# Dense weight units with the low-weight products last, and a mixture-of-experts run that ends without a gather for a step that doesn't follow

## The chip, the cores and the metric

One NeuronCore of a Trainium2 chip. The metric is the device time of one execution in microseconds (us). The engines are TensorE (PE; its weight loads are listed as PEld), VectorE (DVE), ScalarE (ACT), GpSimd (POOL) and SyncE (SP), which issues nearly all DMAs. They run in parallel, each in its own program order, and meet at semaphores only.

## The reference

A trunk of two layers on 256 tokens of 1024 channels, all in float32. Each layer is a token mixer and a channel mixer, both with a norm before and after:

```
h = rms_norm(x, mix_pre_g) * (1 + sc_m) + sh_m
y = hybrid_mixer(h, ...)          # z = h @ w_in; convolution, stick-breaking attention, gated linear attention;
                                  # (g_a * y_a + g_b * y_b + g_c * y_c) @ w_o
x = x + g_m * rms_norm(y, mix_post_g)
h = rms_norm(x, ffn_pre_g) * (1 + sc_f) + sh_f
y = swiglu(h)                     # layer 0: dense, 2816 wide
y = moe_swiglu(h)                 # layer 1: 8 experts, 3584 wide, the best 2 for each token
x = x + g_f * rms_norm(y, ffn_post_g)
```

## The kernel before

**Weights in units.** All weights come from HBM as units of 128 x 2048 floats (1 MB) into six raw buffers, in the fixed order of PLAN for the dense part, then 42 units for each of 8 experts. To reach float32 accuracy with fp32r products, ACT writes the high part of a unit (w_hi, line 592, in the expert part 841) and DVE subtracts it from the raw one for the low part (w_lo, line 990, then 1303). The operand from the activations is split likewise. Every product is then three: high x high, high weights x low activations, low weights x high activations. hi_written counts ACT's parts, raw_taken DVE's (which also frees the raw buffer for SP's next load), consumed counts units that PE has finished (which frees the slot of w_hi and w_lo). There are four slots; the weights of slots 2 and 3 lie in the tensor acts, the others in tensors named w_hi and w_lo.

**The dense part.** PE walks through the units in order. Each takes 48 products (128 x 128 weights, 256 columns), made by project (line 1587), project_tokens (1667), project_branch (1679) or project_down (1697), and each begins with begin(u): wait for raw_taken, then for the PSUM bank. The three products of one chunk follow each other. In each mixer, units 0 to 29 are the columns of w_in, 30 to 35 the outputs of the three branches ("out"), 36 to 39 the columns of w_o ("wo"). The functions hook(layer, i) put the attention, convolution and norm work between units by number. The first eight units of w_in in layer 0 go another way: project_rows (line 1653) runs over all 16 columns with w_hi and high activations, waits, then with w_lo, then with w_hi and low activations.

**Merging the branches.** DVE's merge (lines 1241 and 1245) multiplies each out unit by its gates, POOL adds the first two branches (line 567), and DVE adds the third once POOL's sum is there (line 1245). ACT takes the high part (line 662), DVE the low part (line 1292, counted by s_split). Unit 36 needs both, in four pieces.

**The expert part.** A step is one expert on at most 128 of its tokens. gather(step, half) (line 1994) picks the tokens with a selection matrix that DVE writes (select, line 1395); ACT and DVE split the result (949, 1468). Gate and up units (1959) and down units (1974) follow, the latter summed in banks 5 and 6 over the whole step; turn (1984) transposes the activations, ACT and DVE split them (944, 1461: ae_split). After the last tile of a step PE gathers for the next step, then runs the last two down units. The result is split by ACT and DVE (957, 1476), and scatter (2014, 2015) spreads it back over the tokens in four products p, which DVE adds up (1484). After 8 steps, over_steps (line 464) runs as many more as there are experts with more than 128 tokens; the count is read from memory by every engine, and here it is 0. Then comes the last scatter, ACT's squares (972), their sums on PE (1558), a root (608, 609), and DVE's update of x (1091, 1095), which SP stores.

Of the kernel before, what the change touches and what calls it, by code (L numbers as in the profile page):

```python
# [205 lines left out]
def program(nc, x_t, vecs, c_row, glr_w, a2, router, stream, experts, out_t):  # L206
    with ExitStack() as ctx:
# [152 lines left out]
        first_gate = sem("first_gate_ready")  # L360
        first_high = sem("first_h_high")
# [216 lines left out]
        def _(act):  # L578
# [338 lines left out]
            def expert_step(step, expert, first=False):  # L917
# [20 lines left out]
                for half in range(2):  # L938
                    input_high(step + 1, half)
# [25 lines left out]
            with act.Fori(1, N_EXP) as g:  # L965
                expert_step(g, g)
            n_steps = over_steps(act, expert_step)
# [10 lines left out]
        def _(dve):  # L978
# [507 lines left out]
            def expert_step(step, expert, first=False):  # L1486
# [24 lines left out]
                else:  # L1511
                    dve.wait_ge(list_ready, 1)
                    column = column_of(step + 1)
                select(column, sel, chosen_f, sel_ready)
                select(column, sel_w, weights_f, sel_w_ready)
# [3 lines left out]
                for half in range(2):  # L1519
                    split_input(step + 1, half)  # L1520
# [15 lines left out]
            with dve.Fori(1, N_EXP) as g:  # L1536
                expert_step(g, g)
            n_steps = over_steps(dve, expert_step)
# [6 lines left out]
        def _(pe):  # L1545
# [24 lines left out]
            def begin(u):  # L1570
                pe.wait_ge(raw_taken, POS[u] + 1)
# [5 lines left out]
            def project(u, hi, lo, ready=None, before=0, chunks=1):  # L1577
# [4 lines left out]
                for k in range(KC):  # L1582
                    if ready is not None:
                        pe.wait_ge(ready, before + k // chunks + 1)
                    for c in range(2):
                        for n, (w, high) in enumerate(parts(s)):
# [3 lines left out]
                                           stop=(k == KC - 1 and n == 2), skip_group_check=True)  # L1590
                mm.then_inc(consumed, 1)
# [68 lines left out]
            def project_tokens(u, hi, lo):  # L1660

                s = begin(u)
                out = two(bank[BANKS[u][0][0]])
                for t in range(2):
                    for k in range(KC):
                        for n, (w, high) in enumerate(parts(s)):
                            mm = pe.matmul(out[:, t, :], (hi if high else lo)[:, k, P * t:P * t + P],  # L1667
                                           w[:, 256 * k:256 * k + 256],
# [487 lines left out]
```

## Time and profile before

| | |
|---|---|
| median of 3 runs | 1792.62 us (1791.63 to 1792.68) |
| profiled execution, own time | 1791.98 us |
| its span, first to last instruction | 1790.2 us |
| PE busy | 1761.6 us (98%) |
| DVE busy | 1523.5 us (85%) |
| ACT busy | 1137.0 us (64%) |
| HBM read | 522.65 MB, 293 GB/s over the span |
| mean granted TensorE clock | 0.997 |

The profile is of one execution; times within it count from its first instruction. A busy share says how much an engine has to do; what sets the time is read from the chain that ended last, which is followed back from the last instruction through whatever released it.

### The profile page before, as it was taken

What the parts mean: (1) busy time and instruction counts of PE and PEld (TensorE: products, weight loads), DVE (VectorE), ACT (ScalarE), POOL (GpSimd) and SP (SyncE); (2) the same over time, 40 slices, a digit from 0 to 9 for tenths busy, and PEclk for the clock granted to TensorE, in tenths of its full rate; (3) what the DMA queues carried; (4) which work ended last, traced back from release to release, by engine and by line L of the source; (5) the groups of instructions that cost most, each with busy time, mean ns of one, the idle gap of its engine ahead of it and who ended that gap; (6) DMA issues with size and microseconds to landing.
All of it is one profiled execution on the core that took longest, in us unless ns stands there. A gap on an engine that the chain in (4) does not pass through costs nothing.

```text
span 1790.2 us, 28816 instructions
## 1 busy us (share of the span) xinstructions
PE 1761.6 (98%) x10885; PEld 1560.5 (87%) x10886; DVE 1523.5 (85%) x1450; ACT 1137.0 (64%) x970; POOL 188.3 (11%) x158
## 2 busy tenths in 40 slices
PE   9999999999999999999999999999999999999997
PEld 7999989999999999868888888888888888888886
DVE  7899787999777784769898898898888988988986
ACT  5556475333464556567777777777777777777774
POOL 0395010000029400100000000000000000000000
PEclk9999999999999999999999999999999999999998
DMA  9854655999744444539989989999899899898991
GB/s 387 316 195 154 227 181 199 357 385 371 297 142 165 140 143 142 189 124 362 382 335 364 372 339 369 348 365 372 328 373 374 329 374 370 332 373 338 367 373 73
DMA packets 72818, 524.87 MB, mean 293 GB/s; under 512 B 8145, under 2 KB 8273, under 8 KB 9122
## 3 DMA queue, kind: packets, MB, share of 16 engines
q1 hardware_dynamic: 72578, 523.51, 77.0%
q8 instruction: 59, 0.97, 0.2%
q0 software_dynamic: 160, 0.23, 0.0%
q14 instruction: 21, 0.17, 0.0%
HBM read 522.65 MB, written 1.05 MB: 293 GB/s over the span
## 4 chain that ended last, share of the span: by engine, by line
PE 92%; DVE 5%; ACT 1%; issue 1%; DMA 1%; SPq 0%; DVEq 0%; ACTq 0%
PE bank L1959 34%; PE bank L1587 19%; PE bank L1974 17%; PE bank L1697 4%; PE bank L1679 3%; PE bank L1667 3%; PE bank L1653 2%; PE bank L1994 2%; PE bank L1984 1%; PE bank L1558 1%; DVE w_lo L990 1%; DVE arena L1165 1%; PE bank L1629 1%; DMA raw<-in_stream 1%; PE bank L2014 0%
## 5 line engine op out<-in xcount | busy, mean ns | idle before, releaser
L1303 DVE TENSOR_TENSOR w_lo<-raw,w_hi 128x2048 fp32r<-128x2048 f32 x224 | 509.8, 2291 | 82.6 <-ACT w_hi L841 82.6
L841 ACT ACTIVATE w_hi<-raw 128x2048 fp32r<-128x2048 f32 x224 | 428.6, 1917 | 97.2 <-PE bank L1974 70.4
L1587 PE MATMUL bank<-acts,w_hi 128*128 128x256 f32 x1760 | 311.9, 281 | 7.1 <-DVE acts L1292 3.6
L1959 PE MATMUL bank<-acts 128*128 128x512 f32 x1248 | 304.3, 392 | 0.0
L1959 PE MATMUL bank<-w_hi,acts 128*128 128x512 f32 x960 | 297.3, 391 | 0.0
L1587 PEld LDWEIGHTS bank<-acts,w_hi 128*128 128x128 f32 x1760 | 268.3, 189 | 10.3 <-DVE w_lo L990 6.5
L1303 DVE TENSOR_TENSOR acts<-raw,acts 128x2048 fp32r<-128x2048 f32 x112 | 256.1, 2287 | 20.9 <-ACT acts L841 20.6
L1959 PEld LDWEIGHTS bank<-acts 128*128 128x128 f32 x1248 | 231.2, 188 | 46.8 <-DVE acts L1303 0.4
L841 ACT ACTIVATE acts<-raw 128x2048 fp32r<-128x2048 f32 x112 | 215.1, 1921 | 72.1 <-PE bank L1959 69.8
L1974 PE MATMUL bank<-w_hi,acts 128*128 128x512 f32 x832 | 256.1, 389 | 0.0
L1587 PE MATMUL bank<-acts,w_lo 128*128 128x256 f32 x880 | 245.6, 279 | 0.0
L990 DVE TENSOR_TENSOR w_lo<-raw,w_hi 128x2048 fp32r<-128x2048 f32 x82 | 190.3, 2321 | 44.1 <-ACT w_hi L592 43.8
L592 ACT ACTIVATE w_hi<-raw 128x2048 fp32r<-128x2048 f32 x82 | 156.6, 1911 | 100.4 <-PE bank L1587 70.0
L1959 PEld LDWEIGHTS bank<-w_hi,acts 128*128 128x128 f32 x960 | 178.9, 188 | 36.3
L1959 PE MATMUL bank<-w_lo,acts 128*128 128x512 f32 x480 | 186.8, 389 | 0.0
L1974 PEld LDWEIGHTS bank<-w_hi,acts 128*128 128x128 f32 x832 | 156.2, 188 | 32.4
L1587 PEld LDWEIGHTS bank<-acts,w_lo 128*128 128x128 f32 x880 | 165.7, 188 | 0.0
L1974 PE MATMUL bank<-w_lo,acts 128*128 128x512 f32 x416 | 161.9, 389 | 0.0
L1004 DVE SCALAR_TENSOR_TENSOR raw<-raw,arena 128x1024 f32<-128x1024 f32 x96 | 114.9, 1233 | 15.5 <-DMA raw<-in_stream 10.6
L1959 PEld LDWEIGHTS bank<-w_lo,acts 128*128 128x128 f32 x480 | 90.1, 188 | 19.0
L539 POOL TENSOR_SCALAR arena<-arena 128x256 f32<-128x256 f32 x60 | 102.4, 1707 | 0.0
L1165 DVE SCALAR_TENSOR_TENSOR arena<-arena 128x256 f32<-128x256 f32 x180 | 97.6, 601 | 0.9 <-DVE arena L1215 0.3
(273 smaller groups left out, 2246.0 us busy)
## 6 DMA issues: line engine op xcount, KB each, us to landing
raw<-in_experts SPq DMA_DIRECT2D x336, 1024.0 KB, 5.1
raw<-in_stream SPq DMA_DIRECT2D x161, 1024.0 KB, 6.1
arena<-in_x_t SPq DMA_DIRECT2D x2, 512.0 KB, 4.6
out_t<-arena SPq DMA_DIRECT2D x4, 256.0 KB, 2.4
arena<-in_vecs SPq DMA_DIRECT2D x1, 224.0 KB, 5.4
arena<-in_glr_w POOLq DMA_DIRECT2D x2, 64.0 KB, 4.7
arena<-in_a POOLq DMA_DIRECT2D x2, 32.0 KB, 5.2
arena<-in_router POOLq DMA_DIRECT2D x1, 32.0 KB, 2.1
```

Source lines behind the costliest of these rows:

```text
L539: pool.tensor_scalar(product, src, w, None, ALU.mult).then_inc(pool_products, 1)
L592: act.activation(w_hi[SLOT[u]], raw[:, slot, :], ACT.Copy).then_inc(hi_written, 1)
L841: act.activation(expert_hi[s], raw[:, slot, :], ACT.Copy).then_inc(hi_written, 1)
L990: dve.tensor_tensor(w_lo[SLOT[u]], raw[:, POS[u] % RAW, :], f32(w_hi[SLOT[u]]), ALU.subtract).then_inc(raw_taken, 1)
L1004: ins = dve.scalar_tensor_tensor(w, w, 1.0, cond[row], ALU.mult, ALU.mult, accum_out=ar[:, at:at + 1])
L1165: ins = dve.scalar_tensor_tensor(acc, src, w, acc, ALU.mult, ALU.add)
L1303: dve.tensor_tensor(expert_lo[s], raw[:, slot, :], f32(expert_hi[s]), ALU.subtract).then_inc(raw_taken, 1)
L1587: mm = pe.matmul(out[:, c, :], w[:, 256 * k + P * c:256 * k + P * c + P], (hi if high else lo)[:, k, :], start=(k == 0 and n == 0 and c == 0),
L1667: mm = pe.matmul(out[:, t, :], (hi if high else lo)[:, k, P * t:P * t + P], w[:, 256 * k:256 * k + 256], start=(k == 0 and n == 0), stop=( ...
L1697: mm = pe.matmul(out[:, c % 2, :], w[:, 1024 * f + P * c:1024 * f + P * c + P], (ff_hi if high else ff_lo)[t % 2][:, f, :], start=first, s ...
L1959: mm = pe.matmul(bank[b][:, :], (xe_hi if high else xe_lo)[:, c:c + P], w[:, 512 * kk:512 * kk + 512], start=(half == 0 and kk == 0 and n ...
L1974: mm = pe.matmul(bank[5 + d][:, :], (ae_hi if high else ae_lo)[odd][:, c:c + P], w[:, 1024 * f + 512 * d:1024 * f + 512 * d + 512], start= ...
```

## The change

Five edits:

1. project, project_tokens, project_branch and project_down (but for its last unit) run in two passes over a unit: all products with w_hi first, as soon as hi_written and the bank allow, then, behind the wait for raw_taken, all with w_lo. The number of products and loads is the same.
2. Unit 36 ("wo", first) gets a function of its own, project_merged, which waits for high and low pieces of the activations apart. Units that wait for chunks keep the old order as project_chunks.
3. The last of the 8 expert steps is written out behind the loop, with ahead=False: no selection, no gather and no input split for a ninth step. An overflow step (again=True) gathers for itself at its start.
4. In a step's last down unit the halves d are outermost, and the new semaphore first_half tells ACT when bank 5 is done, so that the first half of the result can be split while PE finishes bank 6.
5. scatter waits for the two halves of the split result one by one, and the last scatter (final=True) has no wait for a next input.

```diff
+            def begin_high(u):
+                pe.wait_ge(hi_written, WPOS[u] + 1)
                 for b, before in BANKS[u]:
                     if before:
                         pe.wait_ge(bank_read[b], before)
                 return SLOT[u]
+            def begin(u):
+                pe.wait_ge(raw_taken, POS[u] + 1)
+                return begin_high(u)
+
+            def low_last(u, hi, lo):
+
+                s = SLOT[u]
+                yield w_hi[s], (hi, lo), True
+                pe.wait_ge(raw_taken, POS[u] + 1)
+                yield w_lo[s], (hi,), False
...
+            def project(u, hi, lo):
+
+                begin_high(u)
+                out = two(bank[BANKS[u][0][0]])
+                for w, parts_of_h, first in low_last(u, hi, lo):
+                    for k in range(KC):
+                        for c in range(2):
+                            for n, h in enumerate(parts_of_h):
+                                mm = pe.matmul(out[:, c, :], w[:, 256 * k + P * c:256 * k + P * c + P], h[:, k, :],
+                                               start=(first and k == 0 and n == 0 and c == 0),
+                                               stop=(not first and k == KC - 1), skip_group_check=True)
+                mm.then_inc(consumed, 1)
+
+            def project_merged(u, hi, lo, before):
+
+                s = begin(u)
+                out = two(bank[BANKS[u][0][0]])
+                for q in range(4):
+                    for n, (w, h) in enumerate(((w_hi[s], hi), (w_lo[s], hi), (w_hi[s], lo))):
+                        if n == 0:
+                            pe.wait_ge(merged_hi, before + q + 1)
+                        if n == 2:
+                            pe.wait_ge(s_split, before + q + 1)
+                        for k in (2 * q, 2 * q + 1):
...
@@ down
-                for f in range(2):
+                order = [(f, d) for f in range(2) for d in range(2)]
+                if last and half == 1:
+                    order = [(f, d) for d in range(2) for f in range(2)]
+                for f, d in order:
...
+                    if last and half == 1 and f == 1 and d == 0:
+                        mm.then_inc(first_half, 1)
                 mm.then_inc(consumed, 1)
@@ scatter
-            def scatter(step):
-
-                pe.wait_ge(ye_split, step * 2)
-                pe.wait_ge(xe_split, step * 2 + 2)
+            def scatter(step, final=False):
+
+                if not final:
+                    pe.wait_ge(xe_split, step * 2 + 2)
                 for p in range(4):
+                    if p % 2 == 0:
+                        pe.wait_ge(ye_split, step * 2 + (p // 2 - 1))
@@ expert_step on TensorE
-            def expert_step(step, expert, first=False):
+            def expert_step(step, expert, first=False, again=False, ahead=True):
+                if again:
+                    gather(step, 0)
+                    gather(step, 1)
...
-                gather(step + 1, 0)
-                gather(step + 1, 1)
+                if ahead:
+                    gather(step + 1, 0)
+                    gather(step + 1, 1)
...
-            with pe.Fori(1, N_EXP) as g:
+            with pe.Fori(1, N_EXP - 1) as g:
                 expert_step(g, g)
-            scatter(over_steps(pe, expert_step))
+            expert_step(N_EXP - 1, N_EXP - 1, ahead=False)
+            scatter(over_steps(pe, over_step), final=True)
@@ expert_result on ScalarE
-                act.wait_ge(consumed, step * EU + N_W)
                 for half in range(2):
+                    if half == 0:
+                        act.wait_ge(first_half, step)
+                    else:
+                        act.wait_ge(consumed, step * EU + N_W)
```

## Rows read from the trace of the kernel before

**Rows 1.** The page: busy time by engine, and the chain's shares by engine.

```profile
PE 1761.6 (98%) x10885; PEld 1560.5 (87%) x10886; DVE 1523.5 (85%) x1450; ACT 1137.0 (64%) x970; POOL 188.3 (11%) x158
...
PE 92%; DVE 5%; ACT 1%; issue 1%; DMA 1%; SPq 0%; DVEq 0%; ACTq 0%
```

**Rows 2.** Windows: us, busy us (instructions) by engine, granted clock, DMA.

```profile
222.00:265.00 43.00, 39.21 (x337) 38.31 (x335) 35.18 (x35) 29.91 (x25) 7.66 (x4) 1.00 0.54 187
320.00:472.00 152.00, 152.00 (x1285) 152.00 (x1284) 141.90 (x170) 54.62 (x36) 0.00 (x0) 1.00 0.97 375
...
800.00:1762.00 962.00, 962.00 (x4528) 803.39 (x4527) 860.81 (x548) 702.69 (x474) 0.00 (x0) 1.00 0.92 355
1771.20:1776.40 5.20, 3.13 (x17) 3.13 (x18) 3.35 (x5) 3.72 (x6) 0.00 (x0) 0.78 0.02 6
```

**Rows 3.** Chain that ended last, 228 to 266 us: start, us, what.

```profile
232.96 0.38 issue
...
244.47 0.84 issue
...
262.73 2.30 DVE w_lo L990
```

**Rows 4.** The same chain, 705 to 745 us.

```profile
722.77 0.42 issue
...
741.39 2.30 DVE w_lo L990
```

**Rows 5.** Timeline of DVE, 244 to 262 us: start, us, instructions, [idle before].

```profile
246.52 2.90 DVE L990 TENSOR_TENSOR w_lo<-raw,w_hi 128x2048 fp32r<-128x2048 f32 x1
...
251.04 0.69 DVE L1241 TENSOR_TENSOR arena<-bank,arena 128x512 f32<-128x512 f32 x1 [0.43 <-PE bank L1679]
...
260.14 1.47 DVE L1292 TENSOR_TENSOR acts<-arena,acts 128x512 fp32r<-128x512 f32 x2
```

**Rows 6.** Instructions of lines 567 and 1245: ns min/median/max, first and last start.

```profile
L567 POOL TENSOR_TENSOR arena<-arena x8: 1292/1300/3345, 246.0 to 729.7; 128x512 f32<-128x512 f32 x8
...
L1245 DVE TENSOR_TENSOR arena<-arena x8: 691/692/1848, 251.8 to 738.2; 128x512 f32<-128x512 f32 x8
```

**Rows 7.** Chain, pieces of three dense stretches.

```profile
27.37 17.18 PE bank L1653 x144
...
203.98 10.91 PE bank L1587 x96
...
323.68 11.31 PE bank L1587 x96
```

**Rows 8.** Timeline, 1755 to 1775 us.

```profile
1758.40 1.10 DVE L1395 TENSOR_SCALAR arena<-arena 128x128 f32<-128x128 f32 x4
...
1759.02 1.92 ACT L841 ACTIVATE w_hi<-raw 128x2048 fp32r<-128x2048 f32 x1 [0.80 <-PE bank L1974]
...
1761.62 2.28 DVE L1303 TENSOR_TENSOR w_lo<-raw,w_hi 128x2048 fp32r<-128x2048 f32 x1
...
1763.83 0.68 DVE L1461 TENSOR_TENSOR acts<-bank,acts 128x512 fp32r<-128x512 f32 x1
...
1771.85 1.29 DVE L1476 TENSOR_TENSOR acts<-bank,acts 128x512 fp32r<-128x512 f32 x2 [4.77 <-ACT acts L957]
```

**Rows 9.** Chain, 1755 to 1791 us.

```profile
1762.14 3.57 PE bank L1994 x32
1765.71 5.48 PE bank L1974 x24
...
1776.40 4.07 PE bank L1558 x16
```

**Rows 10.** Timeline of weight loads, 1770 to 1775 us.

```profile
1773.27 0.19 PEld L2014 LDWEIGHTS bank<-selection_turned,acts 128*128 128x128 f32 x1 [2.51 <-issue]
```

**Rows 11.** Instructions of line 465: ns min/median/max, first and last start.

```profile
L465 PEldq COMPARE_BRANCH  x1: 3372/3372/3372, 1768.0 to 1768.0; - x1
...
L465 DVEq COMPARE_BRANCH  x1: 63/63/63, 1767.3 to 1767.3; - x1
```

More of the change, by code:

```diff
@@ L360, in program @@
         first_gate = sem("first_gate_ready")
+        first_half = sem("expert_first_half")
         first_high = sem("first_h_high")
@@ L915, in silu_tile, with over_step @@
                 act.activation(silu_e[odd], bank[2 * odd][:, :], ACT.Silu).then_inc(silu_done, 1)
-            def expert_step(step, expert, first=False):
+            def over_step(step, expert):
+                expert_step(step, expert, again=True, ahead=False)
+            def expert_step(step, expert, first=False, again=False, ahead=True):
+                if again:
+                    for half in range(2):
+                        input_high(step, half)
                 for k in range(4):
@@ L937, in expert_step @@
                 tile_high(step, 0, FT - 1)
-                for half in range(2):
-                    input_high(step + 1, half)
+                if ahead:
+                    for half in range(2):
+                        input_high(step + 1, half)
             def tile_high(step, odd, t):
@@ L1484, in add_result, with over_step, expert_step @@
                     dve.tensor_tensor(to, to, SCATTER[p][:, :], ALU.add).then_inc(moe_added, 1)
-            def expert_step(step, expert, first=False):
+            def over_step(step, expert):
+                expert_step(step, expert, again=True, ahead=False)
+            def expert_step(step, expert, first=False, again=False, ahead=True):
+                if again:
+                    column = column_of(step)
+                    select(column, sel, chosen_f, sel_ready)
+                    select(column, sel_w, weights_f, sel_w_ready)
+                    for half in range(2):
+                        split_input(step, half)
                 for k in range(4):
@@ L1518, in expert_step @@
                 split_tile(step, 0, FT - 1)
-                for half in range(2):
-                    split_input(step + 1, half)
+                if ahead:
+                    for half in range(2):
+                        split_input(step + 1, half)
             def tile(step, r, rounds, t, whole):
@@ L1575, in begin, with project_chunks @@
                 return SLOT[u]
-            def project(u, hi, lo, ready=None, before=0, chunks=1):
+            def begin(u):
[6 more added lines that the diff above has]
+                yield w_lo[s], (hi,), False
+            def project_chunks(u, hi, lo, ready, before):
                 s = begin(u)
@@ L1582, in project @@
                 for k in range(KC):
-                    if ready is not None:
-                        pe.wait_ge(ready, before + k // chunks + 1)
+                    pe.wait_ge(ready, before + k + 1)
                     for c in range(2):
@@ L1893, in _ @@
                     elif u[2] == 0:
-                        project(u, h_hi, h_lo, s_split, 4 * layer, 2)
+                        project_merged(u, h_hi, h_lo, 4 * layer)
                     else:
@@ L2016, in scatter, with expert_step @@
                     mm.then_inc(scattered, 1)
-            def expert_step(step, expert, first=False):
+            def expert_step(step, expert, first=False, again=False, ahead=True):
+                if again:
+                    gather(step, 0)
+                    gather(step, 1)
                 for k in range(2):
@@ L2051, in tile, with over_step @@
                 turn(step, odd, t)
+            def over_step(step, expert):
+                expert_step(step, expert, again=True, ahead=False)
             pe.wait_ge(htok_copied, 2)
```

106 lines of the change are left out of this document (61 added, 45 removed).

## The prediction, made before the changed kernel was run

> **What bounds the kernel now.** I read the page first: TensorE (PE) is busy 98% of the span and 92% of the chain that ended last lies on it [rows 1]. So only time that PE stands still, or work that it no longer does, can count. Next the windows by stage: the dense feed-forward stretch (320 to 472 us) and the expert stretch (800 to 1762) have no idle PE at all, while 222 to 265, where layer 0 projects and merges its branches, has 3.8 us of it (layer 1 has the same stretch from 700 on), and the tail after 1771 has 2.1 us in 5.2, at a granted clock of 0.78 [rows 2]. The two branch stretches and the tail are the whole field for this change; the chain there says what each stall waits for.
>
> **Part 1: low weights last (project, project_tokens, project_branch, project_down).** Counts stay: 48 products a unit, the same loads, the same DMAs. What moves is the wait for raw_taken (VectorE has subtracted w_lo): from the head of a unit to behind 32 of its 48 products. At 118 ns each [rows 7] that is 3.8 us of cover for a subtraction of 2.3. So a unit that stood waiting for w_lo alone starts when w_hi is there. In the feed-forward stretch nothing waits, and nothing is gained. Behind the new wait in PE's queue stand 16 products and then the next unit; ACT waits for those to free w_hi, at the same point as before.
>
> Where PE waits for w_lo alone: layer 0 has 0.38 us before unit 32, 0.84 before 34, and 2.30 before 37 [rows 3]; layer 1 has the like of the first, 0.42 before 34 and 2.30 before 37 [rows 4]. (A stall near 311 us waits for a PSUM bank that is read behind the same subtraction; it stays.)
>
> Units 32 and 34: PE gets 1.2 us ahead in layer 0, 0.8 in layer 1. The one who must use it is VectorE, whose merge of unit 34 waited only 0.43 us for PE [rows 5]; before that it was busy. So at most 0.43 of the 1.2 is real. And what follows it there is contested: the merge's addition L1245 takes 0.69 us alone and 1.85 at worst, POOL's addition L567 1.30 alone and 3.35 at worst [rows 6], and a w_lo subtraction beside POOL took 2.90 instead of 2.28 [rows 5]: each stands still while the other runs. A merge that comes 0.4 us earlier falls into POOL's third addition in both layers. Its two additions then wait some 0.5 and 0.6 us for POOL. In layer 0 they waited 0.4 in all, so the merge ends -0.43 + 1.1 - 0.4 = 0.25 us later; in layer 1 one of them waited 1.16 (1.85 less 0.69), so it ends 0.45 earlier. Bounds: 0.8 later and, if all that PE gains arrives, 1.2 and 0.8 earlier. The Trainium skill, "SBUF — State Buffer", section "SBUF: two separate sides", says that the port pair shared by VectorE and GpSimd is an exclusive lock for whichever starts first. By that rule part 1 comes out as below, 4.8 us; without it the 0.43 would arrive in both layers, for 5.5. The rows show the lock.
>
> project_merged (unit 36): it now starts on w_lo and the first high quarter and needs each low quarter 8 products later. The last low quarters come from L1292, 1.47 us for two from 260.14 [rows 5]; the unit's products after the last of them fall from 12 to 4, so it ends 0.9 us sooner, at 263.0 in layer 0. Unit 37 is then gated by w_hi, which is ready when its subtraction starts (262.73), not by that one's end (265.03): 2.30 less 0.25 is 2.05. In layer 1: 2.30 and 0.45, 2.75. Bounds: 1.5 each if the lock costs 0.8; 3.5 and 3.1 if everything that PE gains upstream arrives. w_lo of 37 ends 2.3 us after its start and is needed 3.8 after it; then comes w_lo of 38, which also has time. From there the norms are one serial chain and the next stretches are PE's, so it arrives at the end. **Sum of part 1: 4.8 us, bounds 3.0 and 6.6.**
>
> Pace: the chain holds three paces for one and the same loop: 10.91 us for 96 products (113.6 ns), 11.31 (117.8), and the zk units of L1653, which already run all high-weight products, then low, in blocks with a wait between, 17.18 for 144 (119.3, with one slot whose weights lie in acts) [rows 7]. That is the range of the other units, so I cost the new order at nothing; a unit that no longer starts from a stall may run at 117.8 instead of 113.6: 0.2 us for each such unit on the path, 0.2 us on my sum.
>
> **Part 2: no gather for no step.** Step 7 loses 32 gather products, 3.57 us on the chain [rows 9], and on VectorE four selections, 1.10 us [rows 8]. The gather covered a wait: PE's last two down units need the activations' low part, L1461, which began at 1763.83 [rows 8]. VectorE's queue ahead of it: two w_lo subtractions. Without the selections the second starts when ACT's high part is there, 1759.02 + 1.92 = 1760.94, not at 1761.62: 0.66 us earlier. L1461 ends at 1763.85; PE, idle from 1762.14, starts at 1763.9 where the chain has 1765.71. The first product of a rested queue comes out some 0.3 us late. Down units 5.48 us: they end at 1769.65 instead of 1771.20. **1.5 us, bounds 1.3 and 1.8.** ACT and VectorE also lose two input pieces each, off the path.
>
> **Part 3: the last result by halves.** In the last down unit the order turns to d outside, f inside: bank 5 is finished 6 products (1.4 us) before bank 6; ACT's copy and VectorE's subtraction of its half, some 0.6 and 0.7 us, lie under them. The second half is ready 1.3 us after the last product, where both needed 1.94 (1771.85 + 1.29 less 1771.20) [rows 8, 9]. In the steps before the last this changes nothing, since PE has two gate units in between. But PE's own sequencer comes in: it runs the branch over the overflow steps (L465), which takes 3.37 us on PE and 0.06 on the others, from 1768.0 [rows 11], 3.5 us after it was let past L1461. Moved along, it ends near 1770.75, 1.1 us after the down units; the first half can't be scattered before. Then 16 products at 0.12 us: 1772.65. VectorE's four additions (0.69 each) end near 1774.1, the last square at 1774.7, and the sums (L1558), which took 4.07 us partly at the low clock, start with the first square at 1772.7 and end between 1776.1 and 1776.7. Before: 1776.40 + 4.07 = 1780.47 [rows 9]. With 1776.3 the tail gives 4.2 us in all, parts 2 and 3 together; bounds 3.0 (an idle place costs the clock, below) and 4.8 (the branch short). After that ACT's root and VectorE's last updates are the same. The Trainium skill, "Runtime: NRT & Kernel Launch", section "Instruction fetch mechanics", says that a taken branch to a target outside the fetched pages stalls until it is fetched. By it the branch keeps its cost, since the body skipped only grows; the row agrees, with 3.37 us. If instead it were short, the tail would give 0.4 more.
>
> **Sum:** 4.8 - 0.2 + 4.2 = 8.8 us. The profiled execution took 1791.98 us (span 1790.2 and 1.8 around it), so 1783.2; it lies 0.64 below the median of the runs, 1792.62. For the median: **1783.8 us**.
>
> **Rivals.**
> 1. *The dense gain doesn't arrive.* VectorE and POOL take back what PE gains, also at unit 37. For it: the lock [rows 6] and VectorE's 0.43 us. Against: the 2.30 us before unit 37 are on the chain, behind all of POOL's additions. Tail alone: 1792.62 - 4.2 = 1788.4.
> 2. *All of it arrives:* 6.6 + 4.8 = 11.4: 1781.2. It needs POOL to yield and the branch to be short.
> 3. *The clock falls.* After 2.51 us of idle PE [rows 10] the tail's window had 0.78 granted [rows 2]: for a while it was at 1.2 GHz, the lower of its two levels. The scatter took 3.13 us (1773.27 to 1776.40) for 16 products that take 1.9 at full clock, and the sums perhaps 0.6 more. The new order has 1.75 us idle before the last down units and 1.1 behind them, and some 2 us before unit 36. One fall costs 1.2 to 1.8 us, so 1785.2. For it: the idle time is not less, only cut in pieces. Against: the clock stood at 1.00 (2.4 GHz) over 222 to 265, with 3.8 us idle in several pieces [rows 2].
> 4. *Slower: the new order slows the products.* In the chain's rows like those of rows 7 I count 33 units near 113.5 ns, 41 near 117.8, all with weights in w_hi, and 27 at 120 with weights in acts. If all went to 120, the first would lose 0.3 us each, the second 0.1: about 14 us over the sum above, so 1798. It outweighs the gain from a mean of 1.8 ns on each of the 101 x 48 products (8.8 us). For it: the trace shows that the pace isn't fixed by the code. Against: L1653's blocks [rows 7].
>
> **How the numbers follow.** The forecast, 1781.9 to 1785.3 by itself (part 1 between 3.5 and 6, the tail between 3.7 and 4.6): 0.58; rival 1: 0.14; rival 2: 0.09; rival 3: 0.15; rival 4: 0.04. The range takes in rivals 1, 2 and 3: 1780.8 to 1788.7. 0.2% is 3.6 us (the bound for all three chances): faster means below 1789.0. All cases but rival 4 are below; half of rival 4 is slower, some of it and the far end of rival 1 the same: faster 0.92, same 0.06, slower 0.02.
>
> **What would show it.** Right: no wait for w_lo before units 32, 34 and 37 in either layer; PE's idle time in the two branch stretches down by some 2 and 3 us; the dense feed-forward stretch without idle PE and as long as now; in the tail, idle PE of 1.7 us before the last down units, the scatter starting about 1.1 us after them, and from the sums' end to the span's end 9.7 us as now. Wrong: a pace above 118 in the w_hi slots; L1245 waiting longer for POOL; a mid-unit gap in a dense unit (w_lo later than 3.8 us after w_hi); a long branch somewhere else, as at the end of the loop, now that step 7 is written out behind it.

## The result, and the profile after

| | before | after |
|---|---|---|
| median | 1792.62 us | 1782.48 us (5 runs: 1782.21, 1782.21, 1782.48, 1783.84, 1784.10) |
| ratio of the times | | 0.9949, 95% interval 0.9938 to 0.996 |
| profiled execution: own time, span | 1791.98, 1790.2 us | 1784.10, 1782.4 us |

The change makes the kernel 10.1 us faster by the medians, where 8.8 were forecast. The five times after it fall into two groups 1.6 us apart, and the profiled execution is the slowest of them; it is 7.9 us faster than the profiled one before. The median lies in the lower group because three of the five do.

First the page of the changed kernel (it answers to [rows 1]):

```profile
PE 1757.6 (99%) x10853; PEld 1557.2 (87%) x10854; DVE 1522.5 (85%) x1444; ACT 1136.3 (64%) x968; POOL 185.8 (10%) x158
...
PE 90%; DVE 5%; ACT 2%; issue 1%; DMA 1%; SPq 0%; DVEq 0%; ACTq 0%
```

PE has exactly the 32 gather products less (10853 for 10885 records). The windows by stage (us, busy us and instructions of PE, PEld, DVE, ACT, POOL, then granted clock, DMA share, GB/s) answer to [rows 2]:

```profile
222.00:265.00 43.00, 41.11 (x356) 40.52 (x355) 35.71 (x34) 29.76 (x25) 7.58 (x4) 1.00 0.54 190
320.00:472.00 152.00, 152.00 (x1285) 152.00 (x1284) 141.72 (x175) 56.14 (x36) 0.36 (x1) 1.00 0.97 379
...
1756.90:1758.80 1.90, 0.02 (x1) 0.03 (x1) 1.80 (x2) 0.60 (x1) 0.00 (x0) 1.00 0.00 0
1758.80:1761.00 2.20, 2.19 (x8) 1.84 (x9) 0.00 (x0) 0.00 (x0) 0.00 (x0) 0.84 0.02 7
1761.00:1763.50 2.50, 2.50 (x7) 1.93 (x6) 0.00 (x0) 0.00 (x0) 0.00 (x0) 0.50 0.02 7
1763.50:1766.20 2.70, 2.67 (x12) 1.78 (x11) 0.69 (x1) 0.60 (x1) 0.00 (x0) 0.96 0.02 6
```

The branch stretch of layer 0 has 1.9 us less idle PE. The dense feed-forward stretch has no idle PE, as before, and the same 1285 products in it. New is the tail: PE stands still for 1.9 us, and then the granted clock goes to 0.50 (1.2 GHz) while the last down units run.

The chain from the merge of layer 0 on, and the same place in layer 1 ([rows 3] and [rows 4] show it before):

```profile
260.49 0.61 DVE acts L1304
...
261.15 2.10 PE bank L1652 x16
263.25 11.46 PE bank L1635 x96
...
736.48 2.10 PE bank L1652 x16
738.58 11.45 PE bank L1635 x96
```

The 2.30 us of w_lo ahead of unit 37 are gone: after VectorE's third low quarter (the line from 260.49 on is its end) PE has 2.10 us left of unit 36 (16 products: 4 with that quarter, 12 of the last one) and goes on into unit 37 without a stop. The stops before units 32 and 34 are gone too. What PE still waits for in 222 to 266 us is all in unit 36: 1.6 us for its w_lo, since project_merged begins with the old wait, and 0.2 for a high quarter. The chain from 228 to 261 us, which lay on PE's branch units before, now runs through ScalarE and VectorE.

The timeline of the tail (it answers to [rows 8] and [rows 10]):

```profile
1753.86 1.92 ACT L842 ACTIVATE w_hi<-raw 128x2048 fp32r<-128x2048 f32 x1 [0.80 <-PE bank L2050]
...
1755.81 2.29 DVE L1315 TENSOR_TENSOR w_lo<-raw,w_hi 128x2048 fp32r<-128x2048 f32 x1 [0.34 <-ACT w_hi L842]
...
1756.32 0.60 PE L2062 MATMUL bank<-arena 128*128 128x128 f32 x4
...
1758.02 0.68 DVE L1473 TENSOR_TENSOR acts<-bank,acts 128x512 fp32r<-128x512 f32 x1
1758.78 3.50 PEld L2050 LDWEIGHTS bank<-acts 128*128 128x128 f32 x12 [2.09 <-DVE acts L1473]
```

And its chain (it answers to [rows 9]):

```profile
1758.81 7.38 PE bank L2050 x24
...
1766.83 0.70 DVE acts L1488
1767.54 0.04 issue
1767.58 0.39 PE bank L2094
...
1768.84 3.73 PE bank L1582 x16
```

The last w_lo subtraction starts 5.81 us earlier than before while ACT's part ahead of it starts 5.16 us earlier: the selections' 0.65 us are out of VectorE's way. The down units take 7.38 us instead of 5.48 (the 5.48 count from the end of the gather; a row below has 5.70 for them at full clock after a wait). From the sums' end (1772.57) to the span's end are 9.8 us, as before.

Last, the branch over the overflow steps on PE's sequencer ([rows 11]), and the reading of the count ahead of it:

```profile
L465 PEldq TENSOR_LOAD <-ints x1: 483/483/483, 1760.3 to 1760.3; - x1
...
L466 PEldq COMPARE_BRANCH  x1: 3354/3354/3354, 1761.1 to 1761.1; - x1
```

It still takes 3.35 us, but starts 2.4 us after the wait for the low part was over (1758.70), where it was 3.5 before.

### The profile page after: what moved, and what is told of

Read it like the earlier page. It is cut to its first block, busy times and chain, and to the rows that moved or that the text cites. A ratio compares the mean times of both kernels' runs of the same rounds, so it can differ in the third digit from the quotient of the medians.

```text
span 1782.4 us, 28675 instructions
## 1 busy us (share of the span) xinstructions
PE 1757.6 (99%) x10853; PEld 1557.2 (87%) x10854; DVE 1522.5 (85%) x1444; ACT 1136.3 (64%) x968; POOL 185.8 (10%) x158
## 4 chain that ended last, share of the span: by engine, by line
PE 90%; DVE 5%; ACT 2%; issue 1%; DMA 1%; SPq 0%; DVEq 0%; ACTq 0%
PE bank L2033 34%; PE bank L1635 19%; PE bank L2050 17%; PE bank L1760 3%; PE bank L1717 3%; PE bank L1732 3%; PE bank L2072 2%; PE bank L2062 1%; PE bank L1582 1%; PE bank L1693 1%; DVE w_lo L1002 1%; DVE arena L1177 1%; DVE arena L1253 1%; ACT w_hi L593 1%; DMA raw<-in_stream 1%
## 5 line engine op out<-in xcount | busy, mean ns | idle before, releaser
L1635 PE MATMUL bank<-acts,w_hi 128*128 128x256 f32 x1632 | 200.8, 281 | 1.1 <-DVE arena L1134 1.1
L1635 PEld LDWEIGHTS bank<-acts,w_hi 128*128 128x128 f32 x1632 | 193.8, 189 | 3.2 <-issue 2.7
L1635 PE MATMUL bank<-acts,w_lo 128*128 128x256 f32 x816 | 103.1, 279 | 0.0
L1635 PEld LDWEIGHTS bank<-acts,w_lo 128*128 128x128 f32 x816 | 98.4, 189 | 0.0
L540 POOL TENSOR_SCALAR arena<-arena 128x256 f32<-128x256 f32 x60 | 93.0, 1549 | 0.0
```

The costliest lines, as they stand in the source:

```text
L540: pool.tensor_scalar(product, src, w, None, ALU.mult).then_inc(pool_products, 1)
L1635: mm = pe.matmul(out[:, c, :], w[:, 256 * k + P * c:256 * k + P * c + P], h[:, k, :], start=(first and k == 0 and n == 0 and c == 0), stop ...
```

## The experiments

All are made from the kernel before or after by the edit shown. To see where a difference arises, whatever an execution lost upstream, I use ACT's writes of w_hi as milestones: A, the write at the head of the branch stretch (222.51 and 697.86 in the changed kernel); B, the first write behind the merge (261.06 and 736.40); C, the next one that must wait for PE's "wo" units (275.71 and 745.28). A to B is the merge, B to C units 36 and 37. For the tail, T is the start of the last turn and E the end of the span.

| us | A to B, layer 0 | B to C | A to B, layer 1 | B to C | T to E |
|---|---|---|---|---|---|
| before | 38.62 | 16.97 | 39.39 | 11.01 | 28.7 |
| after | 38.55 | 14.65 | 38.54 | 8.88 | 26.1 |
| dense_only | 38.56 | 14.45 | 38.56 | 8.76 | 28.8 |
| tail_only | 39.42 | 16.78 | 39.40 | 11.02 | 24.4 |
| branch_old | 39.41 | 14.64 | 39.39 | 8.88 | 26.0 |
| merged_old | 38.55 | 15.61 | 38.54 | 10.09 | 24.6 |

Each column is one part of the change, and its value repeats to some 0.2 us where that part is the same, with two exceptions that the rest of the study is about: before's A to B in layer 0, and T to E.

The times of whole runs are a coarser measure. Beside the experiments the kernel before ran 34 times more, and took 1789.68 to 1794.70 us. The ratios' intervals reach 1.6 to 2.5 us to either side, more than most differences between two of the kernels below; these are read from the milestones and from the groups of times.

**dense_only, tail_only: the two halves of the change.**

```diff
 dense_only = before + begin_high, low_last, project, project_tokens, project_branch,
              project_down, project_merged          (edits 1 and 2)
 tail_only  = before + expert_step(N_EXP - 1, ..., ahead=False), first_half, scatter by halves
                                                    (edits 3, 4 and 5)
```

> The kernel before with edits 1 and 2 alone (low weights last, project_merged). Theory (the two parts add, and the dense one is worth what the trace of the changed kernel shows): there ACT's writes of w_hi stand 5.2 us earlier than before from the first norm of the expert layer on, so 1792.6 - 5.2 = 1787.4 us. By my own sum it would be 4.6 us, 1788.0. Rival (part of those 5.2 us needs the new tail to arrive): 1789 or more.

> The kernel before with edits 3, 4 and 5 alone (last step written out, no gather for a ninth step, last result by halves). Theory: in the changed kernel's profiled execution the tail gave 7.9 - 5.2 = 2.7 us while its last down units ran at a granted clock of 0.50 for a while and took 7.4 instead of 5.5 us; at full clock it would be 4.3 to 4.6. So two groups of times: about 1788.1 where the clock stays and 1789.8 where it falls. Rival (the spread of the changed kernel's runs comes from its dense part): one group only, within 0.6 us.

dense_only: 1786.43 us, ratio 0.9967 (0.9955 to 0.9979), 6.0 us faster. tail_only: 1789.75 us, ratio 0.9983 (0.9974 to 0.9992), 2.7 us faster. The losses from 1 add up, 0.0033 + 0.0017 = 0.0050, against 0.0051 for the whole, each known to 0.001: nothing shows that the parts depend on each other. The dense part is worth somewhat more than the 5.2 us that I read out of the changed kernel's profile. tail_only's eleven times spread over 1787.4 to 1790.6 without the two clean groups that I expected: in its profile the last down units ran at full clock (T to E is 24.4), but the clock fell at another place, in the router's stretch behind the norms (windows of tail_only):

```profile
780.00:784.00 4.00, 2.69 (x23) 2.13 (x22) 2.40 (x15) 1.75 (x4) 0.00 (x0) 0.93 0.02 4
784.00:787.00 3.00, 3.00 (x16) 2.94 (x16) 0.26 (x2) 1.02 (x2) 0.00 (x0) 0.52 0.00 0
```

There the untouched code came out 1.2 us longer than in the profile before. Such a fall belongs to no part of the change.

**branch_old, merged_old: inside the dense part.**

```diff
 branch_old:
-                begin_high(u)
-                for w, parts_of_h, first in low_last(u, hi, lo):
-                    for c in range(4):
+                s = begin(u)
+                for c in range(4):
...
+                        for n, (w, high) in enumerate(parts(s)):
 merged_old:
-                for q in range(4):
-                    for n, (w, h) in enumerate(((w_hi[s], hi), (w_lo[s], hi), (w_hi[s], lo))):
+                for k in range(KC):
+                    pe.wait_ge(s_split, before + k // 2 + 1)
```

> The changed kernel with project_branch (units 30 to 35) back in the old order. Theory (VectorE and POOL use only part of PE's lead at units 32 and 34): the changed kernel's merge ends 0.1 us earlier in layer 0 and 0.8 in layer 1, measured against the work upstream, so undoing it costs 0.9 us: 1782.5 + 0.9 = 1783.4. Rival 1 (all of PE's lead of 1.2 and 0.8 us arrives): 1784.5. Rival 2 (nothing of it arrives, the merge is earlier for another reason): 1782.5.

> The changed kernel with unit 36 in the old order, each chunk's three products behind the wait for its low quarter. Theory (unit 36's end gates unit 37, now that w_lo doesn't): 12 products instead of 4 follow the last low quarter, 8 x 118 ns = 0.94 us a layer, less nothing, since w_hi of unit 37 is ready 0.25 us before unit 36 ends; 1782.5 + 1.9 = 1784.4. Rival (unit 37 is gated by w_hi or by something else, so the end of unit 36 doesn't matter): 1782.5 to 1782.9.

branch_old: 1784.85 us, ratio 0.9958. By the milestones undoing it costs 0.86 and 0.85 us, 1.7 in all, so rival 1 is nearly right and my theory is wrong: what PE gains at units 32 and 34 does arrive. But in layer 0 the kernel before had 38.62, as fast as after it. The reason shows in VectorE's timeline. The changed kernel:

```profile
249.68 1.87 DVE L1253 TENSOR_TENSOR arena<-bank,arena 128x512 f32<-128x512 f32 x3
251.59 1.14 DVE L1257 TENSOR_TENSOR arena<-arena 128x512 f32<-128x512 f32 x1
252.65 0.68 DVE L1253 TENSOR_TENSOR arena<-bank,arena 128x512 f32<-128x512 f32 x1
253.36 1.07 DVE L1257 TENSOR_TENSOR arena<-arena 128x512 f32<-128x512 f32 x1
```

The same place in tail_only, whose dense part is that of the kernel before:

```profile
249.88 1.27 DVE L1253 TENSOR_TENSOR arena<-bank,arena 128x512 f32<-128x512 f32 x2
251.78 0.69 DVE L1253 TENSOR_TENSOR arena<-bank,arena 128x512 f32<-128x512 f32 x1 [0.62 <-PE bank L1703]
252.50 1.67 DVE L1257 TENSOR_TENSOR arena<-arena 128x512 f32<-128x512 f32 x1
254.09 0.68 DVE L1253 TENSOR_TENSOR arena<-bank,arena 128x512 f32<-128x512 f32 x1
254.81 0.69 DVE L1257 TENSOR_TENSOR arena<-arena 128x512 f32<-128x512 f32 x1
```

With PE ahead, the third multiplication follows the second at once instead of waiting for PE, and the additions take 1.14 + 1.07 us instead of 1.67 + 0.69. In the profile before, layer 0 had 0.69 and 1.07, the cheapest order of all, and layer 1 1.85 and 0.69 [rows 6]. Both engines' rows for the two layers of the kernel before (VectorE's first addition, and POOL's third and fourth together):

```profile
250.53 3.09 POOL L567 TENSOR_TENSOR arena<-arena 128x512 f32<-128x512 f32 x2
251.77 0.69 DVE L1245 TENSOR_TENSOR arena<-arena 128x512 f32<-128x512 f32 x1
...
728.41 2.54 POOL L567 TENSOR_TENSOR arena<-arena 128x512 f32<-128x512 f32 x2
729.65 1.85 DVE L1245 TENSOR_TENSOR arena<-arena 128x512 f32<-128x512 f32 x1
```

POOL's third addition takes 1.3 us in both, and its fourth starts at 251.78 and 729.66, within some 10 ns of VectorE's first. In layer 0 VectorE runs at once and POOL's takes 1.84 us; in layer 1 POOL runs at once and VectorE's takes 1.85. So the old code has two outcomes 0.8 us apart, depending on who of VectorE and POOL comes first. Of the six places with the old order (both layers of before, tail_only and branch_old) only before's layer 0 went VectorE's way, and the profile on which I forecast held this lucky one. It also shows that these two engines, said at the start to meet at semaphores only, hold each other up without one.

merged_old: 1785.89 us, ratio 0.9962; B to C is 0.96 and 1.21 us longer than after. Layer 0 has the theory's 0.94. In layer 1 the granted clock fell while unit 36 ran, behind 2.3 us of idle PE from 730 us on, and the 0.25 us over layer 0 are most likely its price:

```profile
734.60:738.10 3.50, 3.50 (x19) 3.50 (x18) 3.34 (x6) 1.66 (x3) 0.00 (x0) 0.51 0.69 279
```

The clock fell in the router's stretch too (from 779 on), and the five times are two near 1784.7 and three from 1785.9 to 1786.5; the theory's 1784.4 is the lower group. The median alone would have given the old unit 36 a price of 3.4 us.

**gather_kept, whole_result: inside the tail.**

```diff
 gather_kept:
-            with pe.Fori(1, N_EXP - 1) as g:
+            with pe.Fori(1, N_EXP) as g:
                 expert_step(g, g)
-            expert_step(N_EXP - 1, N_EXP - 1, ahead=False)
...
+                pe.wait_ge(ye_split, step * 2)
 whole_result:
-                order = [(f, d) for f in range(2) for d in range(2)]
-                if last and half == 1:
-                    order = [(f, d) for d in range(2) for f in range(2)]
...
+                pe.wait_ge(ye_split, step * 2)
```

> The changed kernel with edit 3 undone (last step in the loop, with selections, gather and input split for a ninth step), halves kept. Theory (the gather covers a wait for the low part of the activations, of which only the selections' share comes back): the last down units start 1.5 us later than in the changed kernel, 1782.3 + 1.5 = 1783.8, and since PE comes to them from work, no second group of times 1.6 us higher from these units. The branch over the overflow steps ends some 0.3 us after the down units, under the second half's split. Rival 1 (the branch gates the scatter, as I forecast for the changed kernel, by 1.1 us): 1784.9 or more. Rival 2 (the whole 3.57 us of gather count): 1785.9.

> The changed kernel with edits 4 and 5 undone (down order f outside d, no first_half, one wait of the scatter for both halves), still without the gather. Theory: the scatter's first product stands 2.07 us behind the last down product as before, its last one 2.07 + 1.92, where the changed kernel has 1.40 + 0.96: 1.6 us more at full clock; the idle PE of 2.07 us may cost the clock again, up to 1.2 us. So 1783.9 to 1785.1, middle 1784.5. By my sum, in which parts 2 and 3 gave 1.5 and 2.7 us, 1785.0. Rival (the halves gain nothing, since the squares and sums wait for something else): 1782.5.

gather_kept: 1785.10 us (1784.84 to 1785.18), ratio 0.9962, one narrow group. Turn at 1756.55, down units at 1760.47, so 3.92 us where the changed kernel has 2.49 (1756.32 to 1758.81): the gather was worth 1.4 us, and rival 2 falls. The time is still 1.3 us over my 1783.8. Unlike what its expectation says, the kernel kept the scatter's one wait for both halves at its head, and the scatter started at 1767.77, 1.6 us behind the down units; that accounts for about 1.1 us of it (T to E is 26.9, where 24.4 and 1.4 make 25.8). So rival 1's number, 1784.9 or more, came true for another reason: the branch took 3.45 us from 1763.0 and ended at 1766.48, 0.3 us behind the down units (1766.18) as the theory has it, and well ahead of the scatter.

whole_result: 1783.85 us (1783.66 to 1785.97), ratio 0.9957, the changed kernel's two groups again, both 1.5 us higher (1783.7 to 1783.9 and 1785.3 to 1786.0, for 1782.2 to 1782.5 and 1783.8 to 1784.1). So the halves give 1.5 us, the low end of what I expected, and not the 2.7 of my sum, by which it would have been 1785.0. Its profile had the low clock in the down units (7.33 us) and full clock in the scatter and the sums.

**warm: products in PE's idle time.**

```diff
+                if not ahead:
+                    s = moe_begin(step, EU - 2)
+                    for _ in range(8):
+                        pe.matmul(bank[7][:, :], xe_hi[:, 0:P], expert_hi[s][:, 0:512], start=True, stop=True)
                 pe.wait_ge(ae_split, step * FT + FT)
```

> The changed kernel with 8 products more in the last step, into a free bank, between the last turn and the wait for the activations' low part, where PE stands idle for 1.9 us. Their result isn't used. Theory (idle PE there makes the granted clock fall in some executions, and that is the difference of 1.6 us between the changed kernel's two groups of times): the last down units always take 5.5 to 5.7 us; 1782.3, and no time 1.6 us above it from this place (a fall in the router's stretch, 1.2 us, may remain). Rival (the groups come from elsewhere): the spread stays, and the times rise by up to 0.2 us.

1782.28 us (1782.14 to 1782.70), ratio 0.9948: the upper group is gone. Windows of warm over the eight products and the down units:

```profile
1756.50:1758.60 2.10, 2.06 (x11) 1.41 (x9) 1.97 (x2) 0.60 (x1) 0.00 (x0) 1.00 0.01 4
1758.60:1764.30 5.70, 5.65 (x24) 4.37 (x24) 0.69 (x1) 0.61 (x2) 0.00 (x0) 1.00 0.02 4
```

5.7 us at full clock against 7.4, and T to E is 24.3. Five executions alone could miss the upper group by chance (it had two of five in the changed kernel, three of five in no_over below); the fifteen of the three kernels named pieces, which shorten the same idle time, have none either. I made seven profiles of kernels with this idle time of 1.9 us, after itself included. In four (after, branch_old, whole_result, no_over) the down units took 7.3 to 7.4 us, in three (tail_only, merged_old, pool_half) 5.7. The same idle time makes the clock fall in some executions and not in others, and costs 1.6 us when it does.

**no_over: without the branch.**

```diff
         def over_steps(eng, body):
...
-            n = eng.value_load(ints[0:1, 0:1], min_val=0, max_val=3)
-            with eng.If(n > 0):
...
-            return n + N_EXP
+            return N_EXP
```

> The changed kernel without the overflow steps: the count isn't read, no branch, no body, on any engine (with these inputs the count is 0). Theory (in the changed kernel PE's sequencer is let past the wait 24 load and product pairs earlier than it needs and gives them out in 1.5 us, so the 3.35 us branch ends before the down units do): no gain at the tail, 1782.3 to 1782.5. Rival (the branch still gates the scatter by 0.4 to 1.1 us): 1781.2 to 1782.0.

1783.97 us (1782.50 to 1784.37), ratio 0.9953, no gain: three of its five times are in the upper group, and the lower two, 1782.50 and 1782.85, aren't below warm's. T to E is 26.1 with the clock down, as after. The branch costs the changed kernel nothing where the clock falls. Where it stays up, the profiles with the branch have a T to E of 24.3 to 24.6; the 24.6 is merged_old's, whose branch took 3.83 us, ended at 1768.62 with the first half ready at 1768.14, and held the scatter until 1768.79. So it may cost some 0.2 us there.

**pool_half: how much POOL's additions cost the merge.**

```diff
-                    pool.tensor_tensor(m, m, gates[:, 2 * q:2 * q + 2, :], ALU.add).then_inc(branch_added, 1)
+                    m1 = merged[:, 2 * q:2 * q + 1, :]
+                    pool.tensor_tensor(m1, m1, gates[:, 2 * q:2 * q + 1, :], ALU.add).then_inc(branch_added, 1)
```

> The changed kernel with POOL's four additions in each merge over 256 of the 512 columns (the other half is left out, so the result isn't the reference's). Theory (VectorE and POOL stand still while the other runs): in the changed kernel a w_lo subtraction of 2.3 us takes 3.1 and two additions of 0.69 take 1.14 and 1.07 in this stretch, 1.6 us of VectorE's time a layer; with additions half as long half of it comes back, and with it the merge and unit 36: 0.8 us a layer, 1782.3 - 1.6 = 1780.7. Rival (the merge is bound by PE's last branch units, and what VectorE loses is hidden): 1782.3.

1780.38 us (1779.85 to 1781.56), ratio 0.9934; A to B is 37.40 and 37.39, 1.15 us shorter in each layer, where the theory had 0.8. VectorE's timeline in pool_half:

```profile
250.92 0.91 DVE L1258 TENSOR_TENSOR arena<-arena 128x512 f32<-128x512 f32 x1
251.75 0.68 DVE L1254 TENSOR_TENSOR arena<-bank,arena 128x512 f32<-128x512 f32 x1
252.47 0.69 DVE L1258 TENSOR_TENSOR arena<-arena 128x512 f32<-128x512 f32 x1
```

The w_lo subtraction ahead of it falls from 3.1 to 2.5 us. In the changed kernel VectorE's merge, not PE, sets the end of the stretch, and POOL's four additions hold it up by at least 1.15 us a layer, since half of their work is still there.

**pieces, pieces_no_over, pieces_early: the next version.** PE waits in the tail for the low part of all four columns of the last tile. Here ACT and VectorE split the tile in two pieces, and PE starts as soon as the first piece's high part is there.

```diff
+                    act.activation(ae_hi[0][:, 0:256], bank[4][:, 0:256], ACT.Copy).then_inc(part_high, 1)
+                    act.activation(ae_hi[0][:, 256:512], bank[4][:, 256:512], ACT.Copy).then_inc(ae_hi_done, 1)
...
+                        groups = [(d, f, w, ae_hi) for d in range(2) for f in range(2) for w in (hi, lo)]
+                        groups += [(d, f, hi, ae_lo) for d in range(2) for f in range(2)]
...
 pieces_early, besides:
+            n_over = over_count(pe)
             expert_step(N_EXP - 1, N_EXP - 1, ahead=False)
```

> The changed kernel with the last tile's activations split in two pieces of 256 columns in the last step, and the last but one down unit taking all products with their high part first. PE then stands idle for some 0.4 us after the last turn instead of 1.9. Theory (two parts): the clock no longer falls there, so one group of times; and the down units start and end 1.5 us earlier, but now the branch over the overflow steps ends some 1.0 us behind the moment at which the first half is ready and gates the scatter, so that only 0.85 of the 1.5 us arrive: 1782.3 - 0.85 = 1781.45. Rival 1 (the branch costs nothing): 1780.8. Rival 2 (the last products are bound by the split of the low part as before): 1782.3.

> The kernel pieces without the overflow steps: no count, no branch, no body on any engine. Theory (the branch gates the scatter once the down units come sooner): 0.65 us less than pieces, 1780.8, where taking the branch away from the changed kernel itself gained nothing. Rival (it is hidden in both): same as pieces.

> The kernel pieces with the count of overflow steps read on PE before the last step instead of behind it, so that only the branch itself (3.4 us) stands behind the last down units, not the 0.8 us of reading and checking the count. It computes everything. Theory: the branch ends at about the moment at which the first half is ready; all of the 1.5 us arrive: 1780.8. Rival (the register read ahead of the step costs PE's queue more than it saves, or the branch still gates): 1781.4 or more.

1781.27 us (1780.88 to 1781.65), 1781.65 (1780.93 to 1781.67) and 1781.18 (1780.75 to 1781.46); ratios 0.9938, 0.9938 and 0.9937 (0.9924 to 0.9951). The upper group is gone here as well. Chain of pieces:

```profile
1757.08 0.39 ACT acts L949
...
1757.51 4.39 PE bank L2091 x18
...
1762.55 0.70 DVE acts L1494
1763.26 0.61 issue
1763.87 0.38 PE bank L2133
```

and its branch:

```profile
L467 PEldq COMPARE_BRANCH  x1: 3809/3809/3809, 1759.9 to 1759.9; - x1
```

The first half is ready at 1763.24; PE starts the scatter at 1763.87, right behind the branch, which took 3.81 us and ended at 1763.7. Now it does gate. But I mis-sized what that costs: the second half is ready 1.36 us after the first, and the scatter's second part waits for it anyway. In pieces_early the branch ended at 1762.6 and the scatter began at 1763.30; from the last turn to the sums it took 9.32 us (1756.60 to 1765.92), in pieces 9.45 (1756.60 to 1766.05). pieces_no_over, without any branch, took 9.32 too. So the branch costs pieces 0.13 us, not 0.65, and the three medians don't tell the kernels apart. pieces_early computes everything and is 1.3 us faster than the changed kernel by the medians; measured against the kernel before, the intervals of the two overlap (0.9924 to 0.9951, 0.9938 to 0.996).

## Why the prediction was right, and where not

The total came out 1.3 us better than forecast. The waits that were to go did go; two terms were mis-sized, the merge in part 1 and the halves in part 3, and the clock was left out of the comparison on one side.

**Part 1, 4.8 us.** The mechanism held, and the terms at units 36 and 37 did to 0.2 us: I had 2.30 a layer behind the merge, B to C gave 2.32 and 2.13. What was mis-sized is the merge itself, "ends 0.25 us later" in layer 0 and "0.45 earlier" in layer 1. It ended 0.07 and 0.85 us earlier. I had PE's lead land in POOL's third addition and cost two waits; in fact those waits (1.14 - 0.69 and 1.07 - 0.69) are 0.8 us together, less than the 1.1 I gave them and than the one wait of 1.16 in layer 1 before, and PE's lead comes on top. And layer 0's profile held an order of VectorE and POOL that the same code doesn't always get. Part 1 is 5.4 us by the milestones of the two profiles (0.07 + 2.32 + 0.85 + 2.13), and 6.0 from tail_only's to the changed kernel's (0.87 + 2.13 + 0.86 + 2.14), which is also what dense_only gained. The rule of the Trainium skill, "SBUF — State Buffer", section "SBUF: two separate sides", the exclusive lock, agrees with the four rows above (one engine's addition runs in its own time, the other's takes 1.84 or 1.85 us) and with pool_half; that it speaks for 4.8 and against the lead was my use of it. Of the signs, PE's idle time from A to C fell from 3.9 to 1.9 us in layer 0 and from 4.1 to 1.9 in layer 1, where I had 2 and 3; the rest of the 3.0 us that layer 1 gained is busy time, 45.5 us for 46.3 with the same 394 products, and why these ran faster isn't shown.

**Pace.** The 96 products behind unit 36 took 11.46 and 11.45 us. At 119 ns each they are above the 118 that I named as a sign of being wrong, but the chain before has 11.68 and 11.48 for the same 96, and the feed-forward stretch holds 1285 products in 152 us before and after: rival 4 has nothing for it. 0.3 us that the changed kernel lost ahead of milestone A (222.51 for 222.17) are not seen in dense_only (222.18), so they are no effect of the order.

**Part 2, 1.5 us.** 1.4 from gather_kept. The profile before says the same: from the turn's start to the first product of the down units it had 3.93 us (1761.54 to 1765.47), the changed kernel 2.49.

**Part 3 and the whole tail, 4.2 us.** T to E fell from 28.7 to 24.3 or 24.4 us at full clock, 4.3. But gather_kept gives 1.4 of it and whole_result 1.5, 2.9 together. The other 1.3 to 1.4 us are the clock, and they are in the 28.7: the kernel before has a fall of its own. PE waits 2.1 us for the split result, and in the scatter behind that wait the step from product to product goes from 0.12 to 0.21 us (chain of the kernel before):

```profile
1773.65 0.12 PE bank L2015
...
1774.27 0.21 PE bank L2014
```

Scatter and sums took 3.13 + 4.07 us there, and 2.17 + 3.73 in whole_result, which has the same wait and order but kept full clock at this place: 1.3 us. dense_only, with the old tail, has the fall as well (2.71 + 4.54 us, granted clock 0.50 over 1768.9 to 1770.3). No profile with the result split by halves has it. My sum took the 16 products at 0.12 us and the sums' end at 1776.3, so it counted on the clock's return; what it called part 3, 2.7 us, is 1.5 for the halves and some 1.3 for a clock that no longer falls there. At equal clock the tail is worth 2.9 us, not 4.2. Whether the kernel before has this fall in every execution isn't shown: both profiles of the old tail have it, and one of dense_only's six times, 1785.10, lies 1.2 us below the others.

One step of it was wrong, without harm: the branch doesn't hold the scatter for 1.1 us. In the changed kernel the first scatter product stands at the down units' end (1766.19 after 1758.81 + 7.38), since with the low clock that end came late; in warm, at full clock, it stands at 1764.68, 0.4 us behind. The error was to move the branch along with the wait as a block: PE's sequencer gave out the 24 pairs of the written-out step in 1.6 us (1758.70 to 1760.3), where it had needed 2.7 in the loop, with the gather's products ahead of them (1764.51 to 1767.2). In warm the scatter is held for these 0.4 us by the branch (the first half was ready at 1764.25), but its first part ends at 1765.6, just as the second half is ready, so nothing is lost. The Trainium skill's rule of a taken branch out of the fetched pages ("Runtime: NRT & Kernel Launch", section "Instruction fetch mechanics") fits PE's 3.35 to 3.83 us. VectorE's and ScalarE's branches over their own bodies took 0.06 and 0.05 us; why these don't stall no run shows.

**Rival 3, the clock.** It isn't a case beside the forecast but a toss within it. I gave one fall 1.2 to 1.8 us; it is 1.6, in two of the five runs. So the changed kernel should have 1791.98 - 5.4 - 4.3 = 1782.3 us without it and 1783.9 with it, and the groups lie there. My 1783.8 came about from too small a dense gain (0.6 us), 0.2 us for a pace that didn't change, 0.6 us of mismatch between the profiled execution before and its median, and no fall. That the median is the 1782.48 of the lower group and not 1783.84 is luck: one more fall in five would have done it, and the forecast would have looked exact.

**Rivals 1 and 2.** Rival 1 is out: the dense gain arrives. Of rival 2 the dense half is nearly right: 1.7 of the 2.0 us that PE gains at units 32 and 34 arrive (branch_old), and the dense part is 5.4 to 6.0 us of its 6.6. Its other half, 0.6 us from a short branch, is out, since the branch costs 0.2 us at most. The 10.1 us by the medians lie halfway between my 8.8 and its 11.4.

## What to carry to other kernels

Before an engine's lead is written off because the next engine is contended, look at the same code in another execution: an order decided by some 10 ns can be worth 0.8 us, and one profile shows one side. Before two tails are compared, look at the granted clock in both: here the one before had it down for a while, and 1.3 of the 4.3 us were that. Where a stage of PE ends in a wait of some 2 us, the wait can have a second price, the clock after it, and here it was paid only sometimes; a spread of the times in two groups was its sign, and products in the idle time or an earlier start took both away. A wait on a whole tile is best cut where its parts are ready at different times; and work that gates nothing today, like the branch here, gates as soon as the work before it gets shorter.

## What the runs showed of the hardware that I had not expected

- The granted clock fell to 0.50 after 1.9 us of idle PE in four of seven profiles of kernels with the same code there; after the router's waits in two of fourteen (tail_only, and merged_old, 3.00 us at 0.51 from 779 on), at 1.2 us; behind the 2.1 us wait ahead of the old scatter in two of three (before and dense_only, not whole_result), at 1.3 us; and in merged_old's unit 36 in layer 1.
- VectorE's addition of 0.69 us and POOL's of 1.3 us, started within some 10 ns of each other, don't share: one keeps its time and the other takes 1.85 us, and it was VectorE in one layer and POOL in the other.
- One and the same forward branch over a body that isn't run takes PE's sequencer 3.35 to 3.83 us from kernel to kernel (twelve profiles), and the other engines 0.05 to 0.06.
- PE's sequencer gave out load and product pairs at some 65 ns each in the written-out last step and near 110 in the loop. The loop also had the gather's products still ahead of it, and no run separates the two.
